# A two-block transformer kernel: both layers' up projections as seven products of half blocks, with the first layer's weight sums made by DMA during its mixer

## The chip, the cores and the metric

The kernel runs on one core of a Trainium2 chip. The metric is the device time of one execution in microseconds (us). In what follows PE is the matrix engine (TensorE), PEld its weight loads, DVE the vector engine, ACT the scalar engine, POOL the GpSimd engine and SP the queue engine that issues most DMAs. POOL can issue DMAs too, and only its DMAs can add to what already stands in memory.

## The reference

Two transformer blocks run one after the other on a sequence of 512 tokens with 1024 features, in float32. The first block's mixer is a stick-breaking attention beside a gated convolution, the second's an HGRN2 recurrence beside a sliding-window attention. Both end in the same kind of feed-forward part:

```
h = rms_norm(x, norm2_g)                                   # 512 x 1024
gate, val = split(h @ w_up)                                # 1024 x 2816 each; second block: w_gate_2, w_up_2
gate = silu(causal_depthwise_conv(gate, ffn_dw_w, b))      # three taps along the tokens
x = x + (gate * val) @ w_down                              # 2816 x 1024
```

The output is the RMS norm of the second block's x.

## The kernel before, in words

**Products.** To keep float32 accuracy each operand is split into a high and a low part, and each product is three matmuls (high by high, high by low, low by high). Activations are held with features on the partitions and 512 tokens along the row.

**Units.** Weights pass through the kernel as a row of "units", each 128 x 1024 numbers (512 KB). For a unit u, SP loads it into `w_raw` (two units make a pair of 1 MB; there is room for four units), ACT copies it to the high part (`lead`, line 744), POOL subtracts to get the low part (`rest`, line 610; a few are DVE's, line 1292), and PE multiplies. SP may load unit u only when the rest of unit u - 4 is done, and ACT may write its high part only when PE has used unit u - 4. `U_IN`, `U_OUT`, `U_UP`, `U_DOWN` number the first unit of the first layer's input projection (20 units), output projection (8), up projection and down projection (22); the names with a 2 are those of the second layer. Each engine's instructions run in the order in which they are written, so every wait holds all that is behind it on that engine.

**Up projection.** The 2816 columns of gate and of value are done in 11 steps of 256 columns. A plain step has four units and 96 matmuls with 512 columns streamed each. A step of the other kind (`sevenfold`) takes the gate and the value together: it splits tokens and features in halves, forms four sums of weight blocks and four sums of activation blocks, and needs seven products of half size instead of eight. It has seven units and 7 x 24 = 168 matmuls with 256 columns streamed. `NC` says how many of a layer's 11 steps are plain: 11 in the first layer and 1 in the second. `NS` is the number of the others.

**Weight sums.** The sums of weight blocks depend on weights alone. They are made in memory by 32 DMAs that POOL issues (`block_sums(step)`): for each of four quarters of the columns (`PIECES`) four plain copies (kinds 0 to 3) and then four DMAs that add (kinds 4 to 7), 1.44 MB written by each. Before each, POOL waits until the step before it has landed (`s_prep`). They are issued one after every second unit from `U_UP + 4` on, in the first layer's up and down projections.

**Activation sums.** The four sums of activations (`cross`, line 1508, on DVE) come from xT, the residual stream, times the norm's gain. ACT splits off their high parts (`cross_hi`, line 936) and DVE the low parts (`cross_lo`, line 1516). They are made between the residual additions at the end of the second layer's output projection and the start of its up projection.

**What else the steps touch.** POOL also forms the norms' inverse roots (`inverse_root`, line 645): it waits for DVE's variance, and DVE waits for its result before it can spread the root over the partitions. In the first mixer `inverse_root(1)` stands behind the rests of `U_OUT` to `U_OUT + 3`. Then come `projected` (rests and additions of squares, line 660) and `inverse_root(2)`. In the second mixer POOL writes some masks (line 692 and the lines after it) before the rest of `U_IN2 + 4`. At the start of a down projection DVE makes the low part of the activations (`split_lo`, line 1558), for which PE waits.

## Time and profile before

| | us |
|---|---|
| median of three runs | 1204.54 (1202.6 to 1206.2) |
| the profiled execution's own time | 1203.35 |
| its span, first to last instruction | 1201.5 |
| PE busy | 1169.1 (97%) |
| DVE, ACT, POOL busy | 688.9, 560.1, 531.6 |
| first mixer with its output projection | 0 to 229 |
| first layer's up projection | 229 to 472 |
| its down projection | 476 to 598 |
| second mixer | 603 to 837 |
| second layer's up projection | 840 to 1072 |
| its down projection | 1074 to 1191 |

The profile was taken of one execution. Busy time of PE is a modelled length of the matmuls, which overlap, so the spacing between the starts of matmuls says more than the length of one.

### The profile page before, as it was taken

Reading aid. Unit: us, or ns where it says so; the run is one execution under the profiler, and the core shown is the slowest. Engines: PE = TensorE matmul, PEld = TensorE weight load, DVE = VectorE, ACT = ScalarE, POOL = GpSimd, SP = SyncE. Lnnn points to the kernel's source line nnn. Section 1 sums busy time; section 2 is a strip of 40 time slices with the busy share of each in tenths; the row PEclk is TensorE's granted clock in tenths of the full one; section 3 lists DMA queues with packets and bytes.
Section 4 is the critical chain, followed back from the end, with each engine's and each line's share of the span. In section 5 each row is a group of like instructions: output and inputs, shape, how many; then the busy total and the mean of one; then the engine's idle time right before and its main releaser. Section 6 shows DMA issues by size and latency. Waiting matters only on the chain.

```text
span 1201.5 us, 17233 instructions
## 1 busy us (share of the span) xinstructions
PE 1169.1 (97%) x6948; PEld 976.3 (81%) x6948; DVE 688.9 (57%) x979; ACT 560.1 (47%) x881; POOL 531.6 (44%) x288
## 2 busy tenths in 40 slices
PE   7999999999999998999999999999899999999997
PEld 6877768788888886888877767778799999998886
DVE  5999973343332334444574577865956666674444
ACT  6356575333232323232445565655566665652323
POOL 3540033655545454445684220008445555564443
PEclk9999999999999998999989999999999999999999
DMA  5422021268978968867823120213255555642321
GB/s 181 140 78 96 4 70 35 71 231 226 236 242 207 243 234 209 201 243 203 207 57 113 64 71 28 80 37 106 70 169 182 182 187 178 191 162 83 105 89 70
DMA packets 115672, 167.75 MB, mean 140 GB/s; under 512 B 3363, under 2 KB 95882, under 8 KB 115594
## 3 DMA queue, kind: packets, MB, share of 16 engines
q1 hardware_dynamic: 102634, 120.26, 30.2%
q0 software_dynamic: 12800, 46.14, 16.0%
q8 instruction: 55, 0.90, 0.3%
q10 hardware_dynamic: 160, 0.26, 0.1%
q14 instruction: 23, 0.19, 0.0%
HBM read 164.29 MB, written 48.23 MB: 177 GB/s over the span
## 4 chain that ended last, share of the span: by engine, by line
PE 88%; DVE 5%; ACT 3%; issue 1%; POOL 1%; DMA 1%; POOLq 0%; ACTq 0%; DVEq 0%; SPq 0%
PE ps L2294 16%; PE ps L1960 13%; PE ps L1962 13%; PE ps L1961 13%; PE ps L2351 10%; PE ps L2355 10%; PE ps L2049 4%; PE ps L2539 3%; PE ps L2095 1%; DVE act_t L1508 1%; PE ps L2491 1%; PE ps L2080 1%; ACT w_hi L744 1%; PE ps L2410 1%; PE ps L2446 1%
## 5 line engine op out<-in xcount | busy, mean ns | idle before, releaser
L610 POOL TENSOR_TENSOR w_lo<-w_raw,w_hi 128x1024 fp32r<-128x1024 f32 x176 | 445.2, 2532 | 518.2 <-ACT w_hi L744 517.3
L744 ACT ACTIVATE w_hi<-w_raw 128x1024 fp32r<-128x1024 f32 x220 | 231.7, 1055 | 278.7 <-PE ps L1962 84.5
L1960 PE MATMUL ps<-h_hi,w_hi 128*128 128x512 f32 x656 | 261.7, 399 | 3.0 <-DVE h_lo L1347 2.1
L1961 PE MATMUL ps<-h_lo,w_hi 128*128 128x512 f32 x656 | 255.7, 390 | 0.0
L1962 PE MATMUL ps<-h_hi,w_lo 128*128 128x512 f32 x656 | 255.7, 390 | 0.0
L1558 DVE TENSOR_TENSOR tt<-act_t,tt 128x512 fp32r<-128x512 f32 x44 | 97.8, 2232 | 117.1 <-ACT tt L971 117.1
L1960 PEld LDWEIGHTS ps<-h_hi,w_hi 128*128 128x128 f32 x656 | 123.1, 188 | 36.3 <-issue 7.5
L1962 PEld LDWEIGHTS ps<-h_hi,w_lo 128*128 128x128 f32 x656 | 123.1, 188 | 26.2
L1961 PEld LDWEIGHTS ps<-h_lo,w_hi 128*128 128x128 f32 x656 | 123.2, 188 | 24.5 <-issue 0.5
L1565 DVE TENSOR_TENSOR ps<-ps,rbs 128x512 f32<-128x512 f32 x88 | 61.5, 698 | 120.2 <-PE ps L1962 118.9
L2294 PE MATMUL ps<-tt,w_hi 128*128 128x256 f32 x640 | 116.2, 283 | 0.0
L2355 PE MATMUL ps<-tt,w_hi 128*128 128x512 f32 x352 | 110.2, 395 | 4.3 <-DVE tt L1558 4.3
L2351 PE MATMUL ps<-w_hi,tt 128*128 128x512 f32 x352 | 108.5, 389 | 1.6 <-DVE tt L1558 1.6
L2294 PEld LDWEIGHTS ps<-tt,w_hi 128*128 128x128 f32 x640 | 99.8, 192 | 0.0
L2294 PE MATMUL ps<-tt,w_lo 128*128 128x256 f32 x320 | 90.6, 283 | 0.0
L976 ACT ACTIVATE cv<-ps,par 128x512 f32<-128x512 f32 x44 | 34.2, 777 | 118.9 <-DVE ps L1565 84.2
L2355 PEld LDWEIGHTS ps<-tt,w_hi 128*128 128x128 f32 x352 | 67.2, 191 | 18.7 <-issue 4.7
L2351 PEld LDWEIGHTS ps<-w_hi,tt 128*128 128x128 f32 x352 | 66.0, 188 | 15.3 <-issue 1.8
L2355 PE MATMUL ps<-tt,w_lo 128*128 128x512 f32 x176 | 69.3, 394 | 0.0
L2351 PE MATMUL ps<-w_lo,tt 128*128 128x512 f32 x176 | 68.5, 389 | 0.0
L2294 PE MATMUL ps<-h_hi,w_hi 128*128 128x256 f32 x220 | 62.3, 283 | 0.0
L2294 PE MATMUL ps<-h_lo,w_hi 128*128 128x256 f32 x220 | 62.3, 283 | 0.0
(331 smaller groups left out, 1949.3 us busy)
## 6 DMA issues: line engine op xcount, KB each, us to landing
w_raw<-in_w_up SPq DMA_DIRECT2D x23, 1024.0 KB, 6.9
w_raw<-in_w_down SPq DMA_DIRECT2D x22, 1024.0 KB, 4.9
w_raw<-blocks SPq DMA_DIRECT2D x40, 512.0 KB, 3.6
w_raw<-in_w_in SPq DMA_DIRECT2D x19, 1024.0 KB, 5.1
blocks<-in_w_up POOLq DMA_DIRECT2D x12, 1408.0 KB, 10.5
blocks<-in_w_gate POOLq DMA_DIRECT2D x12, 1408.0 KB, 6.3
blocks<-blocks POOLq DMA_DIRECT2D x8, 1408.0 KB, 10.4
w_raw<-in_w_gate SPq DMA_DIRECT2D x20, 512.0 KB, 3.6
```

Source lines behind the costliest of these rows:

```text
L610: pool.tensor_tensor(unit_view(w_lo, at, flat), unit_raw(at, flat), unit_view(w_hi, at, flat).bitcast(F32), ALU.subtract).then_inc(s_lo, 1)
L744: act.activation(unit_view(w_hi, at, flat), unit_raw(at, flat), ACT.Copy).then_inc(s_hi, 1)
L1558: dve.tensor_tensor(lo, act_t[:, k, :], hi.bitcast(F32), ALU.subtract).then_inc(s_alo, 1)
L1565: dve.tensor_tensor(ps[:, bank, :], ps[:, bank, :], rbs[:], ALU.mult).then_inc(s_scaled, 1)
L1960: pe.matmul(ps[:, bank, :], whi, hi, start=first, stop=False, skip_group_check=True)
L1961: pe.matmul(ps[:, bank, :], whi, lo, start=False, stop=False, skip_group_check=True)
L1962: mm = pe.matmul(ps[:, bank, :], wlo, hi, start=False, stop=last, skip_group_check=True)
L2049: mm = pe.matmul(ps[:, bank, :].rearrange("p (s n) -> p s n", n=P), a[:, k, t * P:(t + 1) * P], rhs, start=(k == 0 and n == 0), stop=(k == ...
L2294: mm = pe.matmul(ps[:, bank, 0:NH], weight[:, k, n], a, start=begin, stop=False, skip_group_check=True)
L2351: mm = pe.matmul(ps[:, bank, :], a[:, t * P:(t + 1) * P], w[:, cols], start=st, stop=False, skip_group_check=True)
L2355: mm = pe.matmul(ps[:, bank, :], w[:, m * P:(m + 1) * P], a, start=st, stop=False, skip_group_check=True)
L2539: mm = pe.matmul(ps[:, m % 4, :], w, a[:, at, :], start=(first and k == ks[0] and n == 0), stop=(last and k == ks[-1] and n == 2), skip_gr ...
```

## The change

The first layer gets the seven-product form for ten of its eleven steps too, as the second has it. So 64 sum DMAs are needed instead of 32. Those of the first layer have to be made before its up projection and are issued during the mixer: one each after the rests of `U_IN + 6` to `U_IN + 14`, thirteen after that of `U_IN + 15`, one each after those of `U_OUT` to `U_OUT + 7`, and two after that of `U_UP + 3`. The second layer's are spread over the first layer's up projection (9), its down projection (11) and the second layer's input projection (12). A step now waits for the landing of the step two before it, with two semaphores; a step of kind 7 also waits for the step just before it. SP's first load of a step of the up projection waits for the piece of sums that it reads, no longer for all of them.

The rest is order. ACT now writes the residual stream times the gain (`xg`) and DVE makes each activation sum in one instruction of 128 x 1024 instead of four of 128 x 256, all four after the last residual addition. Their low parts are made inside the first steps. The first seven-product step takes its products in another order (`FIRST_ORDER`), with two of its low parts on POOL instead of DVE. At the end of an up projection the splits of the first activation tiles come earlier, and the first four units of a down projection are loaded one by one.

```
-NC = (11, 1)
+NC = (1, 1)
...
 def on_vector(u):
-    return block_of(u) is not None and block_of(u)[1] in (1, 3, 5)
+    at = block_of(u)
+    return at is not None and at[1] in (1, 3, 5) and at not in ((0, 1), (NS[0], 1))
...
 PIECES = 4
+STEPS = 8 * PIECES
+SUMS_AFTER = {u: 1 for u in range(U_IN + 6, U_IN + 15)}
+SUMS_AFTER[U_IN + 15] = 13
+SUMS_AFTER |= {u: 1 for u in range(U_OUT, U_OUT + 8)}
+SUMS_AFTER |= {U_UP + 3: 2}
+SUMS_AFTER |= {u: 1 for u in range(U_UP + 4 * NC[0] + NB, U_DOWN, NB)}
+SUMS_AFTER |= {u: 1 for u in range(U_DOWN, U_DOWN + KF, 2)}
+SUMS_AFTER |= {u: 1 for u in range(U_IN2, U_IN2 + 12)}
+assert sum(SUMS_AFTER.values()) == 2 * STEPS, sum(SUMS_AFTER.values())
+FIRST_ORDER = (1, 2, 0, 3, 4, 5, 6)
+
+
+def product_order(i, lay):
+
+    return FIRST_ORDER if i == NC[lay] else tuple(range(NB))
...
 
             def up(lay, gate, val, v0, u0):
                 for i in range(NC[lay]):
                     pair(u0 // 2 + 2 * i, cols(gate, 256 * i))
                     pair(u0 // 2 + 1 + 2 * i, cols(val, v0 + 256 * i))
-                if NS[lay]:
-                    sp.wait_ge(s_prep, 16 * 8 * PIECES)
                 for i in range(NC[lay], NUP):
+                    piece = (256 * i + 255) // (DFF // PIECES)
+                    for done in s_prep:
+                        done_steps = STEPS * lay + 8 * (piece + 1)
+                        sp.wait_ge(done, 8 * done_steps)
                     u = u0 + 4 * NC[lay] + NB * (i - NC[lay])
                     n = slice(256 * i, 256 * i + 256)
                     v = slice(v0 + 256 * i, v0 + 256 * i + 256)
-                    for j, src in enumerate((blocks[0, :, n], gate[0, 0:DK, n], gate[0, DK:DM, n], blocks[1, :, n],
-                                             blocks[3, :, n], val[0, DK:DM, v], blocks[2, :, n])):
-                        one_block(u + j, src)
+                    sums = blocks[lay]
+                    halves = (sums[0, :, n], gate[0, 0:DK, n], gate[0, DK:DM, n], sums[1, :, n],
+                              sums[3, :, n], val[0, DK:DM, v], sums[2, :, n])
+                    for at, j in enumerate(product_order(i, lay)):
+                        one_block(u + at, halves[j])
...
             def block_sums(step):
 
-                piece, kind = divmod(step, 8)
-                n = slice(piece * (DFF // PIECES), (piece + 1) * (DFF // PIECES))
+                lay, of = divmod(step, STEPS)
+                piece, kind = divmod(of, 8)
+                gate, val, v0 = ((w_up, w_up, DFF), (w_gate_2, w_up_2, 0))[lay]
+                n0 = piece * (DFF // PIECES)
+                n = slice(n0, n0 + DFF // PIECES)
+                v = slice(v0 + n0, v0 + n0 + DFF // PIECES)
                 top, bottom = slice(0, DK), slice(DK, DM)
-                if step:
-                    pool.wait_ge(s_prep, 16 * step)
+                sums, done = blocks[lay], s_prep[step % 2]
+                if step >= 2:
+                    pool.wait_ge(done, 16 * (step // 2))
+                if kind == 7:
+                    pool.wait_ge(s_prep[0], 16 * (step // 2 + 1))
                 if kind == 0:
-                    pool.dma_start(blocks[0, :, n], w_up_2[0, bottom, n]).then_inc(s_prep, 16)
+                    pool.dma_start(sums[0, :, n], val[0, bottom, v]).then_inc(done, 16)
                 if kind == 1:
-                    pool.dma_start(blocks[2, :, n], w_gate_2[0, top, n]).then_inc(s_prep, 16)
+                    pool.dma_start(sums[2, :, n], gate[0, top, n]).then_inc(done, 16)
                 if kind == 2:
-                    pool.dma_start(blocks[1, :, n], w_gate_2[0, top, n]).then_inc(s_prep, 16)
+                    pool.dma_start(sums[1, :, n], gate[0, top, n]).then_inc(done, 16)
                 if kind == 3:
-                    pool.dma_start(blocks[3, :, n], w_gate_2[0, bottom, n]).then_inc(s_prep, 16)
+                    pool.dma_start(sums[3, :, n], gate[0, bottom, n]).then_inc(done, 16)
                 if kind == 4:
-                    pool.dma_start(blocks[0, :, n], w_up_2[0, top, n], accum_op=ALU.add).then_inc(s_prep, 16)
+                    pool.dma_start(sums[0, :, n], val[0, top, v], accum_op=ALU.add).then_inc(done, 16)
                 if kind == 5:
-                    pool.dma_start(blocks[2, :, n], w_up_2[0, top, n], accum_op=ALU.add).then_inc(s_prep, 16)
+                    pool.dma_start(sums[2, :, n], val[0, top, v], accum_op=ALU.add).then_inc(done, 16)
                 if kind == 6:
-                    pool.dma_start(blocks[1, :, n], blocks[0, :, n], accum_op=ALU.add).then_inc(s_prep, 16)
+                    pool.dma_start(sums[1, :, n], sums[0, :, n], accum_op=ALU.add).then_inc(done, 16)
                 if kind == 7:
-                    pool.dma_start(blocks[3, :, n], blocks[1, :, n], accum_op=ALU.add).then_inc(s_prep, 16)
+                    pool.dma_start(sums[3, :, n], sums[1, :, n], accum_op=ALU.add).then_inc(done, 16)
+
+            steps_done = [0]
+            def sums_after(u):
+
+                for _ in range(SUMS_AFTER.get(u, 0)):
+                    block_sums(steps_done[0])
+                    steps_done[0] += 1
...
@@ -672,12 +716,7 @@
             projected(1, U_OUT + 4)
             inverse_root(2)
             rests(U_UP + 3, 1)
-            for n, u in enumerate(range(U_UP + 4, U_IN2)):
-                rests(u, 1)
-                if n % 2 == 0 and n < 16 * PIECES:
-                    block_sums(n // 2)
-            rests(U_IN2, 2)
-            block_sums(8 * PIECES - 1)
+            rests(U_UP + 4, U_IN2 + 2 - U_UP - 4)
...
+            def gained(m, gcol):
+                act.activation(xg[:, m, :], xT[:, m, :], ACT.Copy, scale=par[:, 0, gcol + m:gcol + m + 1]).then_inc(s_xg, 1)
...
-            def cross(lay, gcol, n):
-
-                base = 4 * (lay if NS[0] else 0)
-                up, down = slice(0, NH), slice(NH, SEQ)
+            def cross(lay, n):
+
+                b11, b12 = xg[:, 0:KH, 0:NH], xg[:, 0:KH, NH:SEQ]
+                b21, b22 = xg[:, KH:KD, 0:NH], xg[:, KH:KD, NH:SEQ]
                 if n == 1:
-                    dve.wait_ge(s_tb, base + KH)
-                else:
-                    dve.wait_ge(s_tf, base + n - 1)
-                for k in range(KH):
-                    g1 = par[:, 0, gcol + k:gcol + k + 1]
-                    g2 = par[:, 0, gcol + KH + k:gcol + KH + k + 1]
-                    m2 = minus[:, KH * lay + k:KH * lay + k + 1]
-                    src, scalar, other = ((xT[:, k, up], g1, b12), (xT[:, KH + k, down], m2, t1f),
-                                          (xT[:, KH + k, up], m2, t2f), (xT[:, KH + k, down], g2, b12))[n - 1]
-                    op = dve.scalar_tensor_tensor((t1f, t2f, t4f, t3f)[n - 1][:, k, :], src, scalar, other[:, k, :],
-                                                  ALU.mult, ALU.subtract)
-                op.then_inc(s_tf, 1)
+                    dve.wait_ge(s_xg, KD * (lay + 1))
+                    dve.tensor_tensor(t1f, b11, b12, ALU.subtract).then_inc(s_tf, 1)
+                if n == 2:
+                    dve.wait_ge(s_tf, 4 * lay + 1)
+                    dve.scalar_tensor_tensor(t2f, b22, -1.0, t1f, ALU.mult, ALU.subtract).then_inc(s_tf, 1)
+                if n == 3:
+                    dve.wait_ge(s_tf, 4 * lay + 2)
+                    dve.scalar_tensor_tensor(t4f, b21, -1.0, t2f, ALU.mult, ALU.subtract).then_inc(s_tf, 1)
+                if n == 4:
+                    dve.tensor_tensor(t3f, b22, b12, ALU.subtract).then_inc(s_tf, 1)
...
-                if NS[lay]:
-                    cross(lay, gcol, 2)
                 spread(rb_n)
-                if NS[lay]:
-                    cross(lay, gcol, 3)
-                    cross(lay, gcol, 4)
-                    for x in range(2, 5):
-                        cross_lo(lay, x)
-                if lay:
-                    dve.wait_ge(s_scaled, 4 * NUP)
+                for x in range(1, 5):
+                    cross(lay, x)
                 dve.wait_ge(s_rb, rb_n)
                 dve.tensor_copy(rbs[:], ps[:, 5, :]).then_inc(s_rbs, 1)
                 dve.wait_ge(s_rbs, lay + 1)
```

The first place is POOL's order in the first mixer, between the rests of the input projection and `inverse_root(1)` (the row of `small`). `w_lo` rows are rests, `s_hi` is ACT's high part, `s_var` DVE's variance. Before, from the rest of `U_IN + 2` on:

```order
L610 TENSOR_TENSOR w_lo<-w_raw,w_hi 128x1024 [waits s_hi,s_lo]
L610 TENSOR_TENSOR w_lo<-w_raw,w_hi 128x1024 [waits s_hi] x13
L610 TENSOR_TENSOR w_lo<-w_raw,w_hi 128x1024 [waits s_hi,s_spl]
L610 TENSOR_TENSOR w_lo<-w_raw,w_hi 128x1024 [waits s_hi] x3
L645 TENSOR_TENSOR small<-small 128x4 [waits s_var]
```

After, the last three of the thirteen sum steps behind the rest of `U_IN + 15` (`s_prep0` and `s_prep1` count landed sum steps with even and odd numbers), and then down to `inverse_root(1)`:

```order
L670 DMA blocks<-in_w_up 512x704 [waits s_prep1]
L672 DMA blocks<-in_w_up 512x704 [waits s_prep0]
L674 DMA blocks<-in_w_up 512x704 [waits s_prep1]
L639 TENSOR_TENSOR w_lo<-w_raw,w_hi 128x1024 [waits s_hi,s_spl]
L676 DMA blocks<-blocks 512x704 [waits s_prep0]
L639 TENSOR_TENSOR w_lo<-w_raw,w_hi 128x1024 [waits s_hi]
L678 DMA blocks<-blocks 512x704 [waits s_prep0,s_prep1]
L639 TENSOR_TENSOR w_lo<-w_raw,w_hi 128x1024 [waits s_hi]
L664 DMA blocks<-in_w_up 512x704 [waits s_prep0]
L639 TENSOR_TENSOR w_lo<-w_raw,w_hi 128x1024 [waits s_hi]
L666 DMA blocks<-in_w_up 512x704 [waits s_prep1]
L689 TENSOR_TENSOR small<-small 128x4 [waits s_var]
```

What moved: sum steps 19 to 25 now stand in these rows, each with a wait for a landing, ahead of the rests of `U_OUT` to `U_OUT + 3` and of `inverse_root(1)`; nineteen more steps stand further up.

The second place is POOL's order where the second layer starts, around `inverse_root(3)` and ahead of the masks (`lmask`). Before:

```order
L610 TENSOR_TENSOR w_lo<-w_raw,w_hi 128x1024 [waits s_hi] x3
L641 DMA blocks<-blocks 512x704 [waits s_prep]
L660 TENSOR_TENSOR htmp<-htmp,sq 128x512 [waits s_sq]
L660 TENSOR_TENSOR htmp<-htmp,sq 128x512 [waits s_acc,s_sq] x6
L645 TENSOR_TENSOR small<-small 128x4 [waits s_var]
L610 TENSOR_TENSOR w_lo<-w_raw,w_hi 128x1024 [waits s_hi,s_diag]
L610 TENSOR_TENSOR w_lo<-w_raw,w_hi 128x1024 [waits s_hi]
L692 MEMSET lmask 128x640 [waits s_used]
```

After:

```order
L674 DMA blocks<-in_w_up 512x704 [waits s_prep1]
L704 TENSOR_TENSOR htmp<-htmp,sq 128x512 [waits s_sq]
L704 TENSOR_TENSOR htmp<-htmp,sq 128x512 [waits s_acc,s_sq] x6
L689 TENSOR_TENSOR small<-small 128x4 [waits s_var]
L639 TENSOR_TENSOR w_lo<-w_raw,w_hi 128x1024 [waits s_hi,s_diag]
L676 DMA blocks<-blocks 512x704 [waits s_prep0]
L639 TENSOR_TENSOR w_lo<-w_raw,w_hi 128x1024 [waits s_hi]
L678 DMA blocks<-blocks 512x704 [waits s_prep0,s_prep1]
L731 MEMSET lmask 128x640 [waits s_used]
```

What moved: a kind 6 step now stands behind the rest of `U_IN2 + 2` and a kind 7 step, with both semaphores to wait for, behind that of `U_IN2 + 3`, ahead of the masks.

## Rows read from the trace of the kernel before

**Rows 1.** The page: busy time of an engine, share, instructions.
```profile
PE 1169.1 (97%) x6948; PEld 976.3 (81%) x6948; DVE 688.9 (57%) x979; ACT 560.1 (47%) x881; POOL 531.6 (44%) x288
```

**Rows 2.** Stretches: from:to, length, busy times, granted clock, DMA share, GB/s.
```profile
250.00:472.00 222.00, 221.95 (x980) 183.45 (x978) 73.68 (x104) 69.99 (x85) 118.95 (x65) 1.00 0.83 235
474.40:481.20 6.80, 4.95 (x12) 3.96 (x13) 6.11 (x8) 0.81 (x2) 1.16 (x1) 0.50 1.06 225
604.10:610.90 6.80, 6.80 (x19) 5.42 (x20) 4.29 (x4) 0.00 (x0) 4.59 (x3) 0.50 0.01 4
1072.00:1192.00 120.00, 118.42 (x524) 97.98 (x524) 57.28 (x40) 36.30 (x55) 51.08 (x24) 1.00 0.25 87
```

**Rows 3.** Timeline of PE, first and last matmul of unit `U_IN2 + 4`: start, length.
```profile
627.87 0.39 PE L1960 MATMUL ps<-h_hi,w_hi 128*128 128x512 f32 x1
...
633.08 0.39 PE L1962 MATMUL ps<-h_hi,w_lo 128*128 128x512 f32 x1
```

**Rows 4.** Chain that ended last, in order of time: the seven-product steps.
```profile
870.89 190.08 PE ps L2294 x1584
```

**Rows 5.** Waits of PE: us in total, times, longest.
```profile
PE ps L2355 <- DVE tt L1558: 4.3, 1, 4.3
PE ps L2116 <- POOL htmp L660: 3.2, 2, 2.4
PE ps L1960 <- DVE h_lo L1347: 2.1, 2, 1.8
...
PE ps L2351 <- DVE tt L1558: 1.6, 1, 1.6
PE ps L2235 <- ACT xT L962: 1.3, 1, 1.3
```

**Rows 6.** The page: DMA queues (packets, MB, share) and issues (KB, us to landing).
```profile
q1 hardware_dynamic: 102634, 120.26, 30.2%
q0 software_dynamic: 12800, 46.14, 16.0%
...
blocks<-in_w_gate POOLq DMA_DIRECT2D x12, 1408.0 KB, 6.3
blocks<-blocks POOLq DMA_DIRECT2D x8, 1408.0 KB, 10.4
```

**Rows 7.** Stretch with an adding sum step alone in flight.
```profile
289.00:295.00 6.00, 6.00 (x29) 4.95 (x28) 2.52 (x4) 2.64 (x4) 3.71 (x2) 1.00 1.06 201
```

**Rows 8.** Timeline of POOL in the first mixer: start, length, idle before and releaser.
```profile
36.07 2.40 POOL L610 TENSOR_TENSOR w_lo<-w_raw,w_hi 128x1024 fp32r<-128x1024 f32 x1 [1.15 <-ACT w_hi L744]
...
85.69 2.38 POOL L610 TENSOR_TENSOR w_lo<-w_raw,w_hi 128x1024 fp32r<-128x1024 f32 x1 [2.90 <-ACT w_hi L744]
158.38 7.08 POOL L610 TENSOR_TENSOR w_lo<-w_raw,w_hi 128x1024 fp32r<-128x1024 f32 x3 [70.30 <-ACT w_hi L744]
...
175.54 1.02 POOL L645 TENSOR_TENSOR small<-small 128x4 f32<-128x4 f32 x1 [7.49 <-DVE small L1324]
```

**Rows 9.** Timeline of SP in the first mixer: pair loads issued from here on.
```profile
29.81 58.71 SPq L482 DMA_DIRECT2D w_raw<-in_w_in  x7
104.35 64.14 SPq L482 DMA_DIRECT2D w_raw<-in_w_out  x4
```

**Rows 10.** Line 482, pair loads, at 284 to 330 us.
```profile
DMA to landing us min/median/max: 7.3/7.9/8.8
```

**Rows 11.** The same line at 600 to 800 us, without sum steps.
```profile
DMA to landing us min/median/max: 4.7/5.1/5.2
```

**Rows 12.** Timeline of POOL where the second layer starts.
```profile
607.34 5.62 POOL L610 TENSOR_TENSOR w_lo<-w_raw,w_hi 128x1024 fp32r<-128x1024 f32 x2 [0.80 <-DVE diag L1319]
612.89 0.63 POOL L692 MEMSET lmask<- 128x640 f32 x1
...
623.62 2.40 POOL L610 TENSOR_TENSOR w_lo<-w_raw,w_hi 128x1024 fp32r<-128x1024 f32 x1
```

**Rows 13.** Chain that ended last, 170 to 200 us.
```profile
180.03 2.99 PE ps L2095 x20
```

More of the change, by code:

```diff
@@ L1026, in sevenfold @@
                     lead(u + 7)
+                    if i == NUP - 1:
+                        for k in range(2):
+                            split_hi(lay, k)
                     tap0_at(0)
@@ L1031, in sevenfold @@
                     if i == NUP - 1:
[L1032 removed]
+                        for k in range(2, 4):
                             split_hi(lay, k)
@@ L1585, in quad @@
                         tap2(i, c, c)
-                    if i == NUP - 1:
-                        for k in range(4):
-                            split_lo(lay, k)
-                    if i == NC[lay] - 1 and NS[lay]:
-                        rest(u0 + 4 * NC[lay] + 1)
+                    if i == 0:
+                        cross_lo(lay, 1)
                     for c in range(2):
@@ L2334, in sevenfold @@
-                for c in range(2):
-                    pe.wait_ge(s_c, 8 * g + c + 1)
-                    product(5, c)
-                wait_lo(pe, u + 6)
-                for c in range(2):
-                    pe.wait_ge(s_qc, 8 * g + 4 + c + 1)
-                    product(6, c)
+                    if j == 2 and first:
+                        pe.wait_ge(s_rbs, lay + 1)
+                        if lay:
+                            pe.wait_ge(s_tc, 8)
+                    elif j == 2:
+                        pe.wait_ge(s_c, 8 * (g - 1) + 4 + 2 * c + 1)
@@ L2342, in down @@
+                for at, j in enumerate(product_order(i, lay)):
+                    wait_lo(pe, u + at)
+                    for c in range(2):
+                        ready(j, c)
+                        product(at, j, c)
             def down(lay, u0):
```

166 lines of the change are left out of this document (83 added, 83 removed).

## The prediction

> **What bounds the kernel now.** I read the busy times first: PE is busy for 97% of the span [rows 1], and in the first layer's up projection 221.95 of 222 us at full clock [rows 2]. There the time is the number of matmuls times their spacing. Then the spacing. Unit `U_IN2 + 4` has 24 matmuls of 512 columns, and from its first to its last start are 23 spacings in 5.21 us, 0.2265 us each [rows 3]. The seven-product steps take 190.08 us for 1584 matmuls of 256 columns, 0.1200 us each [rows 4], so a half-size matmul costs 53% of a full one. Then the waits of PE [rows 5], few and at stage borders. The clock rows show what a wait costs beyond itself: behind the 4.3 us wait at 472 us the granted clock was 0.50 for 6.8 us, behind the 2.4 us wait at 601 us the same, and behind the 1.6 us wait at 1072 us it stayed at 1.00 [rows 2, 5]. Half the 2.4 GHz level for 6.8 us costs 3.4 us of PE work. Last the DMA queues [rows 6], since the change doubles the 46 MB of the sum queue and moves half of it to a stage where POOL is needed on time.
>
> **PE's work.** A plain step is 96 x 0.2265 = 21.74 us, a step of the other kind 168 x 0.1200 = 20.16 us. Ten steps: **-15.8 us**.
>
> **Borders that get better.** The first layer's down projection now starts behind a seven-product step, as the second's does, where the wait was 1.6 us and the clock held. The 4.3 us wait and its 3.4 us of clock go, and at most 1.6 us comes, less with the earlier splits: **-6 us** (bounds -6.1 and -7.7). At the second layer's up projection PE waited 1.8 us for DVE's low part and 1.3 us for ACT's copy of xT [rows 5]. Both stand behind the activation sums, which now come after the last residual addition and no longer ahead of ACT's copy: **-2.5 us** (0 to -3.1).
>
> **The sum DMAs in the first mixer.** The software queue took 16.0% of the span for 32 steps [rows 6], 192 us or 6.0 us a step of all 16 engines' time. A copy lands 6.3 us after its issue, an adding step 10.4 [rows 6]. The difference of 4.1 is data time, so a copy is some 3.9 us and an adding step 8.1 us. While an adding step runs alone, the share is 1.06 [rows 7]: the engines are full, and a second step in flight hides only the start (2.3 us), not the data. The hardware queue took 30.2%, 363 us for 120.26 MB [rows 6], 3.0 us per MB, 3.2 us per pair load.
>
> Now the deadline. POOL's `inverse_root(1)` ran at 175.5 us [rows 8], and DVE and PE wait for its result. In the new order (the first place in the change) it stands behind sum step 25, which waits for the landing of step 23. So three pieces, 24 steps, must have landed: 24 x 6.0 = 144 us of engine time. The first step can be issued when the rest of `U_IN + 6` ends, 36.07 + 2.40 = 38.5 us [rows 8]. In between the engines also carry nine pair loads: the seven of the input projection are issued from 29.8 us on [rows 9], five of them after 38.5, and four of the output projection: 28.5 us. Step 7 of each piece waits for the landing of step 6, and its own start of 2.3 us is then bare. Three times that is 7 us, of which waiting loads fill perhaps half: 3.5. With 2.3 us for the first start, step 23 lands at 38.5 + 2.3 + 144 + 28.5 + 3.5 = 217 us, and with step 25's issue and slack in the first, well-spaced copies `inverse_root(1)` runs at about 219. That is **+43.5 us**. Least: loads fill every gap and hidden starts are perfect, 212, +37. Most: +50. PE has nothing to do in this time, as `spread(1, 6)` stands ahead of all that is left. It comes back at half clock, and the 2.99 us of line 2095 [rows 13] and the mix behind it are on the chain: **+3 us** (0 to 3.4).
>
> What lies ahead is covered. The rests of `U_IN + 12` to `U_IN + 15` get late by up to ten us behind steps 6 and 7, and ACT's high parts too if loads wait, but whatever that costs PE before 175 us is taken out of the same 43.5 us, since POOL's chain of landings does not depend on it.
>
> Here a rule of the Trainium skill speaks against me. "DMA: Bandwidth & Descriptors", section "Anatomy of one DMA — SWDGE (gpsimd) path", fits a DMA from this queue as 2.0 us plus its bytes over 436 GB/s. By it a step of 1.44 MB has 3.3 us of data, and 24 steps with the loads would be done by about 150 us, ahead of the deadline. The trace's 10.4 us for an adding step disagrees, so the sum goes by the trace.
>
> **Start of the first up projection.** Steps 30 and 31 stand behind `inverse_root(2)` and the rest of `U_UP + 3`; step 31 waits 10.4 us for step 30, so the rest of `U_UP + 4` can't come sooner than some 12 us after that of `U_UP + 3`; PE has that long in the plain step. The loads of `U_UP + 6` and on, issued in that time, wait behind them. DVE gets four instructions of 1024 numbers that it hadn't there. I take **+3 us** (0 to 10).
>
> **Second layer's input projection.** In the second place, a kind 6 step is issued behind the first of the two rests, near 610 us of before [rows 12], and lands 10.4 us later. The kind 7 step waits for it and takes 1 us to issue, then the masks start: at 621.5 instead of 612.89 [rows 12]. The rest of `U_IN2 + 4`, done at 623.62 + 2.40 = 626.0, is done at 634.6. PE started that unit at 627.87 [rows 3]. **+6.8 us**, and 3.4 us of clock behind so long a wait: **+10 us** (3 to 13).
>
> **Loads beside adding steps.** In the first up projection four adding steps run while single 512 KB loads are due every 2.9 us. Under such steps a pair load landed after 7.9 us, without them after 5.1 [rows 10, 11]. ACT may write a unit's high part three products ahead of PE's need, 3 x 24 x 0.12 = 8.6 us, of which copy and rest (2.4 us, [rows 8]) leave some 5; an adding step lasts 8.1 us and only one is in flight here: about 1 us each, **+4 us** (0 to 15). The same page, section "Queues, rings and completion order", says that an engine takes turns between its queues packet by packet. By that rule loads would be stretched and not held, and this term would be near 0. The 2.8 us more in the rows is less than a whole adding step, which fits either.
>
> **The sum.** -15.8 - 6 - 2.5 + 43.5 + 3 + 3 + 10 + 4 = +39 us. On the span of 1201.5 us that gives 1240.7, on the execution's own 1203.35 us 1242.5. The median of the runs shown lies 1.2 us above that: 1243.7, **1244 us**.
>
> **The rivals.**
> *Sums hold POOL* (my forecast), 1225 to 1262 us: chance 0.72. For it speaks that 144 + 28.5 us of pure engine time don't fit between 38.5 and 175.5; it turns only if a step costs under 4.4 us on average in place of 6.0.
> *Sums fit*: the other sign. If two steps in flight overlap so that each costs what a copy costs, 3.9 us, the steps end at 38.5 + 2.3 + 24 x 3.9 + 28.5 = 163 us, before the deadline. The -24.3 us stand alone with the 3 us of the start: 1244 - 43.5 - 3 - 10 - 4 = 1183 us. It decides from 4.4 us per step downwards. Against it is the share of 1.06 with one in flight [rows 7]. The page's fit above gives the same outcome. Chance 0.10.
> *Half and half*: the steps take some 5 us on average in pairs, POOL is held some 22 us. With the other terms that is about 1215 us; the chance is 0.05, a fifth of it within 0.3% of before.
> *Loads starve*: with sum steps always queued, an engine stays with the sum queue until it is empty. Then the loads of the units for value and of `U_UP` come only in the bare starts, PE's chain is cut before 175 us (covered), and again behind 240 us, where squares and the second inverse root wait for ACT behind a late load: 15 us at the start of the up projection and 2 to 3 us for each adding step later. 1244 + 12 + 8 = 1264, up to 1290 us. For it are the 7.3 to 8.8 us of [rows 10], against it the page's turn-taking. Chance 0.13.
>
> **How the numbers follow.** The range leaves out *sums fit* and the upper half of *loads starve*: 1214 to 1270 us, my forecast's own being 1225 to 1262. A measurement of this kernel tells 0.3%, 3.6 us, from no change. Faster 0.11 (sums fit, and a little of half and half), same 0.02, slower 0.87.
>
> **What would show it.** PE's longest wait, 30 to 50 us near 178 us, ended by DVE's `diag` behind POOL's inverse root, and POOL idle before its DMAs with DMAs as releasers from some 72 us on. The first up projection some 16 us shorter (about 227 us instead of 243). No 4 us wait and no half clock at the first down projection. A wait of about 7 us at `U_IN2 + 4` released by POOL's `w_lo`. I am wrong if POOL reaches `inverse_root(1)` near 176 us: then adding steps with a second one in flight are cheaper than alone.

## The result

The changed kernel takes **1256.7 us** (median of 4 runs, 1252.5 to 1259.4), the kernel before in the same session 1203.6 us (4 runs, 1202.5 to 1206.2). The ratio is 1.044, 95% interval 1.040 to 1.047: slower, as forecast, and by 53 us where 39 were forecast. The profiled execution of the changed kernel took 1259.4 us, with a span of 1257.6 us; that of before had 1201.5 us.

The page of the changed kernel, its lines for busy times, DMA queues and chain shares:

```profile
PE 1170.1 (93%) x7668; PEld 1009.4 (80%) x7668; DVE 780.6 (62%) x1081; ACT 626.9 (50%) x1007; POOL 572.9 (46%) x322
...
q1 hardware_dynamic: 118858, 135.99, 34.5%
q0 software_dynamic: 25600, 92.28, 29.7%
...
PE 66%; DMA 19%; POOL 5%; DVE 5%; ACT 3%; issue 2%; POOLq 0%; ACTq 0%; DVEq 0%; SPq 0%
```

PE has as much to do as before (1170.1 us beside 1169.1, [rows 1]), though it has 15.8 us less of work: the mean granted clock is 0.967 beside 0.993. The share of PE in the chain that ended last is 66%, and DMAs hold 19% of it. The sum queue took 29.7% for 64 steps: 373.5 us, 5.8 a step, where the forecast had 6.0 [rows 6].

PE's waits (engine, line, who released it, us in total, times, longest):

```profile
PE ps L2055 <- DVE diag L1371: 27.5, 1, 27.5
PE ps L1999 <- DVE h_lo L1399: 7.1, 1, 7.1
PE ps L2443 <- ACT aq L1129: 5.8, 1, 5.8
PE ps L1999 <- POOL w_lo L639: 5.5, 1, 5.5
...
PE ps L2097 <- ACT htmp L852: 4.3, 1, 4.3
PE ps L2333 <- ACT sq L1047: 3.9, 3, 2.2
PE ps L2333 <- POOL w_lo L639: 3.1, 1, 3.1
...
PE ps L2333 <- DVE ps L1643: 2.7, 1, 2.7
PE ps L2388 <- DVE tt L1592: 2.2, 1, 2.2
```

In [rows 5] the longest is 4.3 us. Here 27.5 us stand ahead of the first mixer's `diag` (the diagonal form of the inverse root that DVE makes for PE), and seven others of 2 to 7 us are new. `h_lo` is the low part of an activation, `aq` the queries of the sliding attention, `sq` a buffer that ACT fills, in the seven-product steps with a product's result.

To see where the 56.1 us of span come from, I read the start of the same matmul in both timelines of PE, at the border of each stage:

| PE's matmul | before, us | after, us | shift |
|---|---|---|---|
| first of the second norm's sums (end of first mixer) | 235.92 | 281.56 | +45.6 |
| end of the last up matmul | 471.95 | 516.62 | +44.7 |
| first of the first down projection | 476.25 | 518.83 | +42.6 |
| its end | 598.38 | 640.22 | +41.8 |
| first of the sliding scores | 633.40 | 683.02 | +49.6 |
| first with `pT` (line 2446 before) | 650.2 | 708.4 | +58.2 |
| seven products of the second layer [rows 4] | 870.89 | 925.86 | +55.0 |
| first of the second down projection | 1074.1 | 1127.3 | +53.2 |
| end of the span | 1201.5 | 1257.6 | +56.1 |

There are two places where time is lost, the first mixer (45.6) and 640 to 708 us (16.4), and one where it should have been won and was not, the first up projection (0.9 instead of some 9, its start and loads counted).

The chain that ended last, of the changed kernel, in order of time (start, length, what), from 129 to 282 us:

```profile
129.86 17.20 DMA blocks<-blocks
147.56 0.62 POOL blocks L678
148.18 14.59 DMA blocks<-in_w_up
...
184.51 15.03 DMA blocks<-blocks
200.04 10.19 DMA blocks<-blocks
...
211.18 1.07 POOL small L689
...
250.09 18.55 DMA w_raw<-in_w_up
269.62 0.61 ACT sq L970
...
281.56 0.80 PE ps L2155 x8
```

The chain steps from one sum DMA to the next, with a POOL instruction between them only to issue. `inverse_root(1)` (`POOL small`) comes at 211.18, where it was at 175.54 [rows 8]. The second half is another mechanism: at 250.09 a pair load of `U_UP`'s weights takes 18.55 us to land, and ACT's `sq`, DVE's `h_lo` and, for 7.1 us, PE wait for it. Between the two, the shift grows from 35.6 to 45.6 us.

The same view from 649 to 698 us, at the second layer's input projection:

```profile
652.28 10.64 DMA blocks<-blocks
...
663.42 1.01 POOL blocks L678
...
675.90 2.39 POOL w_lo L639
678.35 15.45 DMA w_raw<-in_w_in
...
697.62 1.23 PE ps L2443 x8
```

First POOL waits for a sum DMA (652.28), the masks and the rest of `U_IN2 + 4` come late; that was forecast. Then a pair load lands 15.45 us after its issue, and PE waits 5.8 us a second time; that was not.

The clock, in stretches of the changed kernel (columns as in [rows 2]):

```profile
213.00:219.00 6.00, 5.79 (x16) 4.03 (x17) 5.18 (x7) 0.00 (x0) 0.00 (x0) 0.51 1.02 396
518.80:522.20 3.40, 3.37 (x9) 2.68 (x10) 3.40 (x7) 0.00 (x0) 2.61 (x1) 0.56 1.01 385
675.40:682.20 6.80, 6.80 (x21) 5.47 (x22) 0.00 (x0) 0.00 (x0) 5.85 (x4) 0.69 0.83 282
```

Behind the 27.5 us wait PE is granted 0.51 (1.2 of 2.4 GHz), behind 2.2 us at the down projection 0.56, behind 5.5 us at 675 us 0.69.

### The profile page after: what moved, and what is told of

Same layout as the page of the kernel before. It is cut to its first block, busy times and chain, and to the rows that moved or that the text cites. A ratio compares the mean times of both kernels' runs of the same rounds, so it can differ in the third digit from the quotient of the medians.

```text
span 1257.6 us, 19149 instructions
## 1 busy us (share of the span) xinstructions
PE 1170.1 (93%) x7668; PEld 1009.4 (80%) x7668; DVE 780.6 (62%) x1081; ACT 626.9 (50%) x1007; POOL 572.9 (46%) x322
## 3 DMA queue, kind: packets, MB, share of 16 engines
q0 software_dynamic: 25600, 92.28, 29.7%
## 4 chain that ended last, share of the span: by engine, by line
PE 66%; DMA 19%; POOL 5%; DVE 5%; ACT 3%; issue 2%; POOLq 0%; ACTq 0%; DVEq 0%; SPq 0%
PE ps L2333 27%; PE ps L2388 9%; PE ps L2384 9%; DMA blocks<-in_w_up 7%; DMA blocks<-blocks 7%; PE ps L1999 4%; PE ps L2000 3%; PE ps L2001 3%; PE ps L2572 3%; POOL w_lo L639 3%; DMA w_raw<-in_w_up 2%; PE ps L2088 2%; DMA w_raw<-blocks 2%; DMA w_raw<-in_w_in 1%; PE ps L2524 1%
## 5 line engine op out<-in xcount | busy, mean ns | idle before, releaser
L2333 PE MATMUL ps<-tt,w_hi 128*128 128x256 f32 x1280 | 232.5, 283 | 4.7 <-ACT sq L1047 3.9
L2333 PE MATMUL ps<-tt,w_lo 128*128 128x256 f32 x640 | 181.1, 283 | 0.0
L1999 PE MATMUL ps<-h_hi,w_hi 128*128 128x512 f32 x376 | 156.7, 417 | 13.6 <-DVE h_lo L1399 7.1
L2000 PE MATMUL ps<-h_lo,w_hi 128*128 128x512 f32 x376 | 150.0, 399 | 0.0
L2001 PE MATMUL ps<-h_hi,w_lo 128*128 128x512 f32 x376 | 149.7, 398 | 0.0
L2333 PE MATMUL ps<-h_hi,w_lo 128*128 128x256 f32 x440 | 125.5, 285 | 0.0
L2333 PE MATMUL ps<-h_lo,w_hi 128*128 128x256 f32 x440 | 125.5, 285 | 0.0
L2333 PE MATMUL ps<-h_hi,w_hi 128*128 128x256 f32 x440 | 125.4, 285 | 0.0
L2333 PEld LDWEIGHTS ps<-tt,w_lo 128*128 128x128 f32 x640 | 122.8, 192 | 0.0
L1344 DVE TENSOR_TENSOR w_lo<-w_raw,w_hi 128x1024 fp32r<-128x1024 f32 x72 | 90.9, 1265 | 13.1 <-ACT w_hi L783 13.0
```

The source lines that it names most:

```text
L1344: dve.tensor_tensor(unit_view(w_lo, at, flat), unit_raw(at, flat), unit_view(w_hi, at, flat).bitcast(F32), ALU.subtract).then_inc(s_lod if ...
L1999: pe.matmul(ps[:, bank, :], whi, hi, start=first, stop=False, skip_group_check=True)
L2000: pe.matmul(ps[:, bank, :], whi, lo, start=False, stop=False, skip_group_check=True)
L2001: mm = pe.matmul(ps[:, bank, :], wlo, hi, start=False, stop=last, skip_group_check=True)
L2333: mm = pe.matmul(ps[:, bank, 0:NH], weight[:, k, n], a, start=begin, stop=False, skip_group_check=True)
```

## The experiments

Each kernel is the changed kernel with the edit shown. Times are medians; each ratio is to the kernel before, run 11 to 21 times beside them (1203.9 to 1204.4 us). Line numbers are those of each kernel's own file.

**1. The borders alone, with plain steps in the first layer.**

```
-NC = (1, 1)
+NC = (11, 1)
-SUMS_AFTER = {u: 1 for u in range(U_IN + 6, U_IN + 15)}
...
+SUMS_AFTER = {u: 1 for u in range(U_UP + 4, U_UP + 4 + 64, 2)}
...
```

> The stage borders as changed, but the first layer's up projection with plain steps as before, its loads in pairs, and 32 sum steps after every second unit as before. Theory: the reordering at the second layer's up projection is worth what the two traces show there, a shift of 58.2 us at the end of the second mixer and 53.2 us at the start of the second down projection, so about 5 us: 1198 to 1201 us. Rival: the reorder brings nothing by itself and the 5 us are slack given back behind the late loads before: 1203 to 1205 us.

In this kernel two 256-column blocks of the second layer's input projection stand in each other's place, which changes what is computed there, not how much. Measured: 1199.9 us beside 1204.3, ratio 0.9963 (0.9951 to 0.9976). The theory's range holds. With the two blocks in their order:

```
-            for n, c0 in enumerate((2560, 2048, 2304, 512, 768, 0, 256, 1280, 1024, 1536, 1792)):
+            for n, c0 in enumerate((2560, 2048, 2304, 512, 768, 0, 256, 1024, 1280, 1536, 1792)):
```

> The kernel with the changed borders and plain steps in the first layer once more, with the two 256-column blocks of the second layer's input projection (columns 1024 and 1280) in the order that goes with its unit numbers. Theory: same work, same time as there, 1199 to 1201 us. Rival: the order of these two loads moves PE's waits at the second mixer: more than 3 us away from 1199.9 us.

Measured: 1200.0 us beside 1204.4, ratio 0.9969 (0.9957 to 0.9981). So the reordered second border is worth about 4.4 us in both. The first down projection has its old border here, with the 4.3 us wait of [rows 5]. What PE now waits for at the second one:

```profile
PE ps L2387 <- DVE act_t L1658: 1.3, 2, 0.8
PE ps L2387 <- DVE ps L1646: 1.1, 1, 1.1
```

These 2.4 us have taken the place of 1.6 us in [rows 5].

**2. The first layer's sum steps left out.**

```
-SUMS_AFTER = {u: 1 for u in range(U_IN + 6, U_IN + 15)}
-SUMS_AFTER[U_IN + 15] = 13
-SUMS_AFTER |= {u: 1 for u in range(U_OUT, U_OUT + 8)}
-SUMS_AFTER |= {U_UP + 3: 2}
...
+                    if lay == 0:
+                        halves = (val[0, DK:DM, v], gate[0, 0:DK, n], gate[0, DK:DM, n], gate[0, 0:DK, n],
+                                  gate[0, DK:DM, n], val[0, DK:DM, v], val[0, 0:DK, v])
...
```

> The changed kernel without the first layer's 32 sum steps: the seven products of the first layer read plain half blocks of the weights in place of the sums, as many bytes (its output leaves the first layer's sums out). The second layer's sum steps stand where they do in the changed kernel. Theory (the sum DMAs hold POOL and the loads): no long wait before the first mixer's diag, POOL's inverse root near 175 us, and time = 1257 - 45.5 (shift at the end of the first mixer) - 12 (missing part of the gain in the first up projection) = about 1198 us, down to 1190. Rival (single loads and the activation sums of the new order slow the first up projection by themselves): still some 12 us lost there, and 1208 to 1215 us.

Measured: 1202.3 us, ratio 0.9988 (0.9976 to 1.0001), 4 us above the theory's range and 6 below the rival's. POOL's timeline has the inverse root back where it was:

```profile
175.62 1.02 POOL L688 TENSOR_TENSOR small<-small 128x4 f32<-128x4 f32 x1 [7.50 <-DVE small L1375]
```

The 32 first-layer steps are worth 54 us of the changed kernel's time. What stays is just as telling: without them, but with ten steps fewer of plain work and better borders, the kernel is no faster than before. PE's waits say why:

```profile
PE ps L2442 <- ACT aq L1128: 6.3, 1, 6.3
PE ps L1998 <- POOL w_lo L637: 5.8, 1, 5.8
```

These two belong to the second layer's sum steps at `U_IN2`. From the first seven-product matmul (254.3 us) to the first down projection (462.0) it takes 207.7 us, where the second layer's ten steps take 201.7: 6 us are lost. They are not lost beside the second layer's sum steps. From 288 to 462 us, with eight of the nine of them, PE is busy 174.00 of 174.00 us. The loss lies ahead, in one wait of 2.6 us for DVE at 280.7 and clock 0.58 for the 7.3 us behind it. DVE has been at work almost without a pause since 253 us, and its instructions are slow there. The low part of an activation sum, 128 x 1024, in the first layer beside POOL's rest, and the same instruction in the second layer while POOL is idle:

```profile
258.74 2.41 POOL L637 TENSOR_TENSOR w_lo<-w_raw,w_hi 128x1024 fp32r<-128x1024 f32 x1 [0.34 <-ACT w_hi L782]
258.84 3.38 DVE L1564 TENSOR_TENSOR tt<-act_t,tt 128x1024 fp32r<-128x1024 f32 x1
...
873.60 1.23 DVE L1564 TENSOR_TENSOR tt<-act_t,tt 128x1024 fp32r<-128x1024 f32 x1 [0.49 <-ACT xT L998]
```

DVE's row ends 1.1 us after POOL's, as if it had begun only then. Of DVE's 80 subtractions of this size in this trace (lines 1564 and 1343) six start while a rest runs on POOL, and take 3.0 to 3.4 us; the other 74 take 1.2. So the rival was right that the new order costs something by itself, about half of the 12 us that it said. This is read from the trace; no run changes this order alone. In the changed kernel the first up projection takes 216.0 us, 14.3 lost.

**3. All steps at their places, but the first layer's adding ones only copy.**

```
-                    pool.dma_start(sums[0, :, n], val[0, top, v], accum_op=ALU.add).then_inc(done, 16)
+                adding = dict(accum_op=ALU.add) if lay else {}
+                    pool.dma_start(sums[0, :, n], val[0, top, v], **adding).then_inc(done, 16)
...
```

> All 32 first-layer sum steps are issued at the same places with the same waits, but the 16 adding ones only copy (the output leaves the first layer's additions out). Theory (data time of the steps is what holds POOL): 24 steps of 3.9 us and 28.5 us of loads end near 167 us, POOL's inverse root runs near 176 us, and the time is 1200 to 1212 us. Rival (it is the number of DMAs in a row and their landing latency of some 6 us, not the adding): the inverse root stays more than 15 us late and the time is 1225 us or more.

Measured: 1204.0 us, ratio 0.9998 (0.9984 to 1.0012). POOL's timeline:

```profile
176.57 1.06 POOL L690 TENSOR_TENSOR small<-small 128x4 f32<-128x4 f32 x1
```

The same number of DMAs behind the same waits, and POOL is 1 us late instead of 35.6. The rival, a cost per DMA, is out. What an adding step has more is time of the DMA engines. The sum queue from 38.6 to 176 us in this kernel (35.52 MB are 24.6 steps), and from 38.8 to 210.3 us in the changed one (34.98 MB, 24.3 steps):

```profile
q0 software_dynamic: 6691, 35.52, 70.3%
...
q0 software_dynamic: 9666, 34.98, 81.7%
```

That is 3.9 us a copy, and 5.8 us for the mix, half of whose steps add, so some 7.7 us for an adding step: two thirds of the time is theirs.

**4. The last twelve steps moved from the second input projection into the second mixer.**

```
-SUMS_AFTER |= {u: 1 for u in range(U_IN2, U_IN2 + 12)}
+SUMS_AFTER[U_IN2 + 17] = 4
+SUMS_AFTER_ROOT = {4: 3, 5: 3, 6: 2}
...
```

> The changed kernel with the last 12 sum steps of the second layer taken from the units U_IN2 to U_IN2+11 and issued behind unit U_IN2+17 (4) and behind POOL's inverse roots 4, 5 and 6 (3, 3, 2), where the DMA share is 0.1. Theory: the shift of 16.4 us that comes between 640 and 700 us is due to these steps, POOL's wait for a DMA and loads held behind them: 1239 to 1244 us, and no wait of PE for POOL at U_IN2+4. Rival: PE is late there for the masks and a norm that it would wait for anyhow, or the steps hold the inverse roots in the new place: 1250 us or more.

Measured: 1235.2 us, ratio 1.0249 (1.0225 to 1.0273), 21.5 us less than the changed kernel and 4 below the range. From the end of the first down projection to the end of the span it has 600.6 us where the changed kernel has 617.4, 16.8 less; the other 5 us lie ahead of the edit, where both kernels are the same, and are most likely the scatter of a kernel whose runs lie 7 us apart. Both waits of PE in that stage are gone. The price of the steps there is 16.8 us. With it experiment 2 adds up: -15.8 (work), -4.4 and -3 (borders), +16.8 (the steps at `U_IN2`) and +6 (DVE in the first up projection) make -0.4 us, measured were -2.0.

**5. One step in flight instead of two.**

```
-                if step >= 2:
-                    pool.wait_ge(done, 16 * (step // 2))
-                if kind == 7:
-                    pool.wait_ge(s_prep[0], 16 * (step // 2 + 1))
+                if step >= 1:
+                    pool.wait_ge(s_prep[1 - step % 2], 16 * ((step + 1) // 2))
```

> The changed kernel with every sum step waiting for the landing of the one before it, so that one is in flight and not two. Theory (two in flight hide only the start of a step, the data of both shares the same 16 engines, and loads of the other queue stand behind the data of all steps in flight): 24 steps of 8.35 us on average from 38.5 us on end near 240 us, POOL's inverse root 1 runs at 238 to 245 us (211 with two in flight), the time is 1280 to 1300 us, and no load lands later than some 12 us after its issue where it was up to 18.6 us. Rival A (two steps in flight only disturb each other): the inverse root stays near 211 us. Rival B (loads take turns with the steps, and land late because the queue's own loads are many): loads still take 15 us and more at worst.

Measured: 1317.0 us (two runs, 1314.9 and 1319.0), 17 above the range. `inverse_root(1)` runs at 266.26 us, 21 us beyond the expected range; rival A is out. POOL's timeline, the end of one piece and the start of the next:

```profile
167.44 1.00 POOL L674 DMA_DIRECT2D blocks<-blocks  x1 [10.23 <-DMA blocks<-in_w_up]
178.70 1.01 POOL L676 DMA_DIRECT2D blocks<-blocks  x1 [10.25 <-DMA blocks<-blocks]
189.12 0.66 POOL L662 DMA_DIRECT2D blocks<-in_w_up  x1 [9.41 <-DMA blocks<-blocks]
195.61 0.65 POOL L664 DMA_DIRECT2D blocks<-in_w_up  x1 [5.83 <-DMA blocks<-in_w_up]
```

In these rows it issues copies 6.5 us apart and adding steps 10.4 to 11.3 us apart, so 13 copies and 12 adding steps end at 38.5 + 84.5 + 131 = 254 us, and loads stand between them for the other 12. The other reading is of the pair loads: DMA to landing, least, median and most, from 36 to 290 us and from 600 to 720 us, in the changed kernel

```profile
DMA to landing us min/median/max: 9.7/15.1/22.7
...
DMA to landing us min/median/max: 4.8/11.8/21.7
```

and with one step in flight

```profile
DMA to landing us min/median/max: 5.0/7.4/11.3
...
DMA to landing us min/median/max: 5.0/7.2/9.7
```

A pair load alone takes 5.1 us [rows 11]. One step in flight adds 2 us in the median and 6 at most, two add 7 to 10 in the median and up to 18. Rival B is out as well: the queue's own loads are the same in both kernels. With copies only (experiment 3) the first stretch has 5.0, 9.5 and 18.6 us, without first-layer steps (experiment 2) 4.9, 5.1 and 5.6. In the seven-product part of the first up projection, where the steps stand 20 us apart, one in flight changes nothing: 14.6 us are lost there, beside 14.3.

**6. All 64 steps, spread anew.**

```
...
+SUMS_AFTER[U_IN + 15] = 3
+SUMS_AFTER |= {u: 1 for u in range(U_OUT, U_OUT + 12)}
+SUMS_AFTER |= {u: 1 for u in range(U_UP + 8, U_UP + 44, 5)}
+SUMS_AFTER |= {u: 1 for u in range(U_UP + 48, U_DOWN, 5)}
+SUMS_AFTER |= {u: 1 for u in range(U_DOWN, U_DOWN + KF, 2)}
+SUMS_AFTER[U_IN2 + 17] = 4
...
```

> All ten seven-product steps and all 64 sum steps, issued at other places: 16 ahead of POOL's inverse root 1, 8 one by one behind the units U_OUT+4 to U_UP+3, the others behind every fifth unit of the first up projection, every second of the first down projection, and the last ones behind U_IN2+17 and the inverse roots 4 to 6 in the second mixer. Theory (the loss is only a matter of what waits on POOL and in the queues behind the steps): 16 x 6.0 + 28.5 us of engine time end near 169 us, the inverse root 1 is not held, no wait for POOL at U_IN2+4, and the time is 1202 (no first-layer sums) less 18 (steps at U_IN2) plus 0 to 12 for the eight steps behind the output projection: 1184 to 1196 us. Rival (64 steps and single loads are too much for the queues wherever they stand): 1205 us or more.

Measured: 1245.6 us, ratio 1.0337 (1.0315 to 1.0360). Missed by 50 us. The inverse root came at 198.22 instead of 175.5, for I had put four adding steps right ahead of it, and the same fault sat in the second mixer, which POOL's timeline shows:

```profile
797.36 1.00 POOL L680 DMA_DIRECT2D blocks<-blocks  x1 [16.35 <-DMA blocks<-blocks]
798.01 1.82 POOL L691 TENSOR_TENSOR small<-small 128x4 f32<-128x4 f32 x1
```

The step of kind 7 stands on POOL for the landing of kind 6 (16.35 us, and 15.27 at 854 us), and the next inverse root behind it. This run alone can't tell whether the places or the number of steps are to blame.

**7. Six seven-product steps, 16 first-layer sum steps.**

```
+NC = (5, 1)
+CUTS = ((1280, 2048, 2816), (0, 704, 1408, 2112, 2816))
+SUMS_AFTER = {u: 1 for u in range(U_IN + 6, U_IN + 15)}
+SUMS_AFTER[U_IN + 15] = 3
...
-                        cross_lo(lay, 1)
+                        for x in range(1, 5):
+                            cross_lo(lay, x)
...
```

All low parts of the activation sums are now made in the plain steps, ahead of the first seven-product step.

> Only the last six steps of the first up projection as seven products, the first five plain; the sums are made for columns 1280 to 2816 alone, in two pieces of 768 columns: 16 sum steps, 12 ahead of POOL's inverse root 1 and 4 behind units of the first up projection; the second layer's 32 steps spread from there to the second mixer, none at U_IN2 to U_IN2+11. Theory: 6 x 1.58 = 9.5 us of PE work, 3 us at the first down projection and 4.4 us of the other borders are kept and nothing is held: 1204 - 17 = 1187 us, 1185 to 1193. Rival (loads beside adding steps cost PE a few us for each step, in the first down projection too): 1197 us or more.

Measured: 1212.4 us, ratio 1.0066 (1.0050 to 1.0081), 19 above the theory's range. Fewer steps, and still above the rival's mark. The chain that ended last begins with the same pattern:

```profile
44.41 15.72 DMA w_raw<-in_w_in
...
75.49 18.94 DMA blocks<-blocks
...
101.40 20.55 DMA w_raw<-in_w_in
```

Nine steps behind nine units, 5.4 us apart, are more than the engines can carry beside the loads; these land after 15.7 and 20.6 us.

**8. The same, with steps 11 us apart or where POOL has nothing else to do.**

```
...
+SUMS_AFTER = {u: 1 for u in range(U_IN + 6, U_IN + 15, 2)}
+SUMS_AFTER[U_IN + 15] = 9
+SUMS_AFTER |= {u: 1 for u in range(U_UP + 4, U_UP + 21, 2)}
+SUMS_AFTER |= {u: 1 for u in range(U_UP + 30, U_UP + 55, 12)}
+SUMS_AFTER |= {u: 1 for u in range(U_DOWN, U_DOWN + KF, 2)}
+SUMS_AFTER[U_IN2 + 17] = 5
+SUMS_AFTER_ROOT = {4: 2, 5: 2, 6: 1, 7: 1}
...
```

> As the kernel with five plain and six seven-product steps, with the sum steps at places where nothing waits on POOL and about 11 us apart: 5 behind every second unit from U_IN+6, 9 behind U_IN+15 (POOL is idle there from 86 to 158 us), 9 behind every second unit of the plain up steps, 3 in the seven-product part, 11 in the first down projection, 11 in the second mixer, the step of kind 7 one place behind that of kind 6. Theory (a sum step costs PE only where POOL, or a load behind two steps in flight, is on PE's chain): POOL's inverse root 1 at 176 us and the second layer's up projection without an earlier hold, so 1204 - 9.5 (PE work) - 6 (borders) + 0 to 6 for loads in the seven-product part = 1189 to 1195 us. Rival (16 more steps cost some 1.5 us each wherever they stand): 1205 us or more.

Measured: **1189.7 us**, ratio 0.9882 (0.9867 to 0.9896), 14.7 us faster than before and inside the theory's range. It has the products, the early low parts and the sum steps of experiment 7; only the places of the steps differ, and they are worth 22.7 us. The page:

```profile
PE 1157.0 (97%) x7380; PEld 985.9 (83%) x7380; DVE 738.6 (62%) x1037; ACT 605.9 (51%) x963; POOL 557.1 (47%) x306
...
q0 software_dynamic: 19200, 71.31, 24.6%
...
PE 84%; DVE 6%; ACT 4%; DMA 3%; issue 2%; POOL 1%; SPq 0%; POOLq 0%; DVEq 0%; ACTq 0%
```

PE's waits:

```profile
PE ps L2157 <- POOL htmp L710: 3.2, 3, 2.0
...
PE ps L2335 <- DVE ps L1650: 1.1, 2, 0.6
```

The sum queue carries 24.6% of the span, half more than in [rows 6], and DMAs have 3% of the chain. Its six seven-product steps take 122.5 us (342.3 to 464.8) where 121.0 are six times 20.16, and PE loses nothing in the first 40 us of them. What the early low parts are worth by themselves, no run tells: none has ten seven-product steps and them.

## Why the prediction was right

The direction, the mechanism and the place of the largest loss were right; 17 us of 56 were missing, and in the largest term two errors cancelled. Term by term, forecast and measured on the profiled spans:

| Term | forecast | measured |
|---|---|---|
| sums hold POOL, clock behind it | +46.5 | +45.6 |
| first up projection: work, start, loads | -8.8 | -0.9 |
| border to the first down projection, and that stage | -6 | -2.9 |
| second layer's input projection | +10 | +16.4 |
| second up entry | -2.5 | -3.2 |
| second down projection | 0 | +1.1 |
| sum | +39.2 | +56.1 |

**Sums hold POOL.** `inverse_root(1)` came 35.6 us late and not 43.5, below the least that I gave (37). Step 23 landed at 210.2 and not at 217. From 38.8 us to then the sum queue took 140 us of engine time (144 forecast), the pair loads 27 (28.5), and some 4 us were left over where I had 5.8 for starts. The inverse root followed 1 us behind the landing, not 2. PE's 4.3 us wait for `htmp`, up to 90.6 us, was covered, as said: of the 35.6 us only 27.5 are left as a wait at `diag`. The rest of the 45.6 came from what the forecast gave to *loads starve*: 7.1 us of PE's wait for `h_lo` behind the load of 18.55 us, and clock 0.59 for the 7.1 us behind it, about 3 us. So the total of this stage is right by luck: 8 us too much for the hold, and some 10 us that I had left out. That the steps are the cause is shown by experiment 2, and that it is their engine time, by experiment 3.

**The Trainium skill's figure for a software-queue DMA.** By the Trainium skill, "DMA: Bandwidth & Descriptors", section "Anatomy of one DMA — SWDGE (gpsimd) path", whose fit is 2.0 us plus the bytes over 436 GB/s, a step of 1.44 MB would take 5.3 us, 3.3 of them data (an estimate from that page), and the steps would have fitted. The traces disagree for both kinds: copies that run one at a time are issued 6.5 us apart and adding ones 10.4 us and more (experiment 5), and their engine time is 3.9 and some 7.7 us (experiment 3). *Sums fit* is refuted by `inverse_root(1)` at 211.18.

**The first up projection.** Two terms belong to it, the start (+3) and the loads beside adding steps (+4, "about 1 us each"). From the spacing of PE's matmuls in the changed kernel: some 4.7 us go at the entry, PE's 3.1 us wait for POOL's `w_lo` at 302.8, behind the steps 30 and 31, and the clock behind it (0.76 for 7.2 us). 5.7 go in the next 35 us, in the 2.7 us wait for DVE and the clock behind it (0.74 for 6.5 us), as in experiment 2. 4.8 go beside adding steps, in waits of 0.6, 2.2 and 1.1 us for ACT's `sq`, the last two in the chain behind single loads that landed after 11.29 and 11.88 us. So the term for the loads was about right in this trace, and the start was mis-sized: +3 forecast, 10.4 measured, just above the bound of 10. I had named DVE's four new instructions there and given them no price beside POOL's rests. Why the adding steps cost nothing in experiments 2 and 3, no run tells. Experiment 4, the same kernel up to there, lost 10.5 us in place of 14.3, so some of this is scatter.

**The queues.** The Trainium skill, "DMA: Bandwidth & Descriptors", section "Queues, rings and completion order", has an engine take turns between its queues packet by packet. Experiment 5 tells more than [rows 10] did: the most that a load takes goes from 11.3 us with one step in flight to 22.7 with two. If turns are taken, they don't keep a load from landing 10 us late in the median. That it waits for most of the data of both steps fits the numbers, but a load can also wait for another load, and no run parts the two. Here a step of my working failed: I had taken the 2.8 us between [rows 10] and [rows 11] as what a load suffers, from a kernel with one step in flight, and the change has two in the mixers. Of *loads starve*, whose chance I gave as 0.13, this part was true.

**Second layer's input projection.** The forecast wait was there: 5.54 us for POOL's `w_lo`, and clock 0.69 behind it. The second wait, 5.8 us for `aq` behind a load of 15.45 us, was missing, as was the clock behind it (0.57 for 7 us). Experiment 4 prices both together at 16.8 us.

**The first down projection.** I said that no 4 us wait and no half clock would be left. The wait was 2.2 us with clock 0.56 for 3.4 us behind it. In experiment 2 it is 1.1 and 0.8 us in two parts. The gain of 6 us was to be had at a border where DVE arrives on time; half of it was.

**What held.** The price of a step: six take 122.5 us in experiment 8, six plain ones would take 130.4. The second up entry: -2.5 forecast, -3.2 in the trace, and the borders together -4.4 us in both kernels of experiment 1. The +1.1 at the second down projection are the 2.4 us of waits inside it in place of 1.6 us ahead of it.

## What to carry to other kernels

Before moving background DMAs, sum their engine time (here 5.8 us a step, 3.2 us a pair load) between the first place and the deadline, and list what stands behind each issue on its engine: the places of the steps alone were worth 22.7 us between two kernels with the same instructions. Look also at what stands beside each other on DVE and POOL: a 1.2 us subtraction on DVE took 3.0 to 3.4 us beside POOL's in experiment 2. Allow as many DMAs in flight as a load of the critical queue can stand to wait for, since with two instead of one the worst load went from 11 to 23 us. And take such a trick only as far as its preparation fits: six steps gained 14.7 us, all ten lost 42 at the better of the two sets of places tried.

## What the hardware showed that I had not expected

A load from one queue lands later the more DMAs of the other queue are in flight: in the median 5.1 us (none, experiment 2), 7.4 (one, experiment 5) and 15.1 (two, the changed kernel) in the first mixer. Copies did this as well: with copies only the worst load took 18.6 us. Two DMAs in flight gained no more than their hidden start: step 23 landed 48 us earlier than one by one (210.2 and 258.2), 2.0 us for each of 24, near the 2.3 us that the prediction took for a start. An adding DMA from DRAM to DRAM that lands in 10.4 us alone took up to 17.7 us in pairs. And DVE's subtraction of 128 x 1024 numbers, 1.2 us by itself, gets nowhere while a rest, the same kind of instruction, runs on POOL: in the traces of the changed kernel and of experiment 2 sixteen of them started during a rest, and every one ended 1.1 us after POOL's, after 1.2 us where the rest was nearly over and after 6.2 where three rests ran in a row.
